# The opening of a hybrid attention layer: adaLN weights in four chunks, x transposed as it lands, small rotary tables

## The reference, cut to what matters

```python
mod = silu(c) @ w_ada + b_ada
shift, scale, gate = split(mod, 3)
h = rms_norm(x, norm_pre) * (1 + scale) + shift
proj = h @ w_in            # q, k, v, z of two attention branches, and gates
qa, ka = rope(qa, positions), rope(ka, positions)
... windowed attention (three dilations), differential attention, gated sum
y = rms_norm(y, norm_post)
return x + gate * y
```

## Time and profile before

| | us |
|---|---|
| median of 3 runs | 888.97 (888.87 to 889.76) |
| profiled execution | 890.7 |
| its span, first to last instruction | 888.9 |

### The profile page before, as it was taken

The page is one execution under the profiler, slowest core; times in us unless marked ns, Lnnn a source line. Parts: engine busy times, 40 slices in busy tenths (PEclk is TensorE's granted clock), DMA queues, the critical chain, the costliest instruction groups (busy, mean ns, idle before and its releaser), DMA issues.

```text
span 888.9 us, 12630 instructions
## 1 busy us (share of the span) xinstructions
PE 817.8 (92%) x4622; PEld 685.9 (77%) x4622; DVE 471.3 (53%) x751; ACT 360.0 (41%) x774; POOL 480.2 (54%) x625
## 2 busy tenths in 40 slices
PE   1679799999999999999997599999999999999997
PEld 0558579788888888889777477887878787888897
DVE  2884577354444545324467567857856644202622
ACT  3343444344444444433444244545555642323410
POOL 2574555344566555427767764646746527746300
PEclk9989899999999999999999699999999999999999
DMA  9774273223233433233443222223221113332521
GB/s 248 199 211 118 69 264 119 84 81 99 89 103 95 119 95 105 66 102 109 126 139 111 80 82 78 60 72 105 63 72 57 63 48 95 113 101 88 196 93 51
DMA packets 92852, 94.87 MB, mean 107 GB/s; under 512 B 8269, under 2 KB 84086, under 8 KB 92662
## 3 DMA queue, kind: packets, MB, share of 16 engines
q1 hardware_dynamic: 92496, 93.64, 34.8%
q0 software_dynamic: 240, 0.39, 0.5%
q10 hardware_dynamic: 54, 0.02, 0.0%
HBM read 78.21 MB, written 5.34 MB: 94 GB/s over the span
## 4 chain that ended last, share of the span: by engine, by line
PE 66%; POOL 9%; DVE 8%; issue 6%; DMA 5%; ACT 4%; SPq 3%; DVEq 0%; POOLq 0%; ACTq 0%
PE proj L1502 46%; POOL w_lo L694 5%; PE score L1381 4%; PE proj L1580 4%; PE sums L1427 3%; PE turned L1398 3%; DMA ada<-in_w_ada 2%; PE score L1356 2%; PE sums L1429 2%; DVE ada_sum L1025 1%; POOL rope_x L719 1%; DVE dstat L1145 1%; ACT junk L923 1%; ACT probs L891 1%; POOL rows_in L752 1%
## 5 line engine op out<-in xcount | busy, mean ns | idle before, releaser
L694 POOL TENSOR_TENSOR w_lo<-raw,w_hi 128x256 fp32r<-128x256 f32 x392 | 319.4, 846 | 218.6 <-ACT w_hi L807 218.3
L1502 PE MATMUL proj<-h_hi,w_hi 128*128 128x512 f32 x608 | 253.2, 416 | 8.3 <-POOL h_lo L704 7.1
L1502 PE MATMUL proj<-h_hi,w_lo 128*128 128x512 f32 x608 | 241.8, 398 | 0.0
L1502 PE MATMUL proj<-h_lo,w_hi 128*128 128x512 f32 x608 | 240.4, 395 | 0.0
L1502 PEld LDWEIGHTS proj<-h_hi,w_hi 128*128 128x128 f32 x608 | 116.3, 191 | 44.4 <-issue 9.9
L1502 PEld LDWEIGHTS proj<-h_hi,w_lo 128*128 128x128 f32 x608 | 116.1, 191 | 26.3
L1502 PEld LDWEIGHTS proj<-h_lo,w_hi 128*128 128x128 f32 x608 | 116.9, 192 | 21.1
L807 ACT ACTIVATE w_hi<-raw 128x1024 fp32r<-128x1024 f32 x100 | 104.2, 1053 | 11.9 <-PE proj L1502 7.7
L719 POOL TENSOR_TENSOR rope_x<-rope_x,cos_t 128x512 f32<-128x512 f32 x36 | 55.0, 1529 | 87.7 <-DMA rope_s<-rope_x 87.7
L1168 DVE TENSOR_TENSOR at_lo<-turned,at_hi 128x512 fp32r<-128x512 f32 x64 | 44.0, 688 | 63.7 <-ACT at_hi L909 63.2
L891 ACT ACTIVATE probs<-score,dstat 128x512 f32<-128x512 f32 x64 | 43.4, 684 | 60.6 <-DVE dstat L1145 60.6
(11 more groups left out here) (245 smaller groups left out, 1531.3 us busy)
## 6 DMA issues: line engine op xcount, KB each, us to landing
raw<-in_w_in SPq DMA_DIRECT2D x88, 512.0 KB, 3.6
rope_s<-rope_x SPq DMA_DIRECT2D x144, 64.0 KB, 2.4
ada<-in_w_ada SPq DMA_DIRECT2D x16, 512.0 KB, 6.3
zd<-in_w_ada SPq DMA_DIRECT2D x8, 512.0 KB, 5.6
raw<-in_w_proj_b SPq DMA_DIRECT2D x8, 512.0 KB, 3.4
raw<-in_w_out SPq DMA_DIRECT2D x8, 512.0 KB, 4.2
rows_in<-window_rows SPq DMA_DIRECT2D x4, 792.0 KB, 4.7
window_rows<-rows_out SPq DMA_DIRECT2D x4, 528.0 KB, 4.9
```

Of the source, the lines that this page charges most:

```text
L694: ins = nc.gpsimd.tensor_tensor(lo[:, k, :], raw[:, n % RAW, k, :], hi.bitcast(F32)[:, k, :], ALU.subtract)
L1502: ins = mm(dst, left, right, start=k == 0 and n == 0, stop=k == nk - 1 and n == 2)
```

## The change: four chunks, early transposes, small tables

- `w_ada` (scale and shift) comes in four chunks of 256 channels, each as eight DMAs of 256 KB in runs of 1 KB, each with its own semaphore. There is memory for all four; the last one lies where x was, so SyncE waits for `x_turned` of all eight rows before it. VectorE adds a 128 x 512 piece per instruction in place, 29 of them; three pieces of chunk 0 go to TensorE as four small matmuls each. The folding is four matmuls per chunk.
- All of x is first on SyncE's queue. Each tile is normalized after its own statistics and its transposes follow at once into seven PSUM banks; rows 2 to 7 are copied to SBUF (`xt`), and ScalarE makes `h_hi` and `h_f` from there.
- After a chunk TensorE does its two rows k for the q and k tiles and, for k 0 to 3, for the four v tiles too, which now live in the two score banks. Of the v tiles, ticks 8 to 11 keep k 4 to 7. The last two rows go pair by pair, and the swap DMAs too.
- Six halves have their own raw slots; block 3 is prepared in the opening, in memory of its own.
- Positions come as 32 frequencies x 4 quarters of 128 positions, so the angle instructions and the Sins are 128 x 128; the tables go out to DRAM and come back in eight DMAs. The lambda vectors go behind the last chunk on SyncE's queue, and their VectorE work moves to the head of ticks 12 and 24.
- G_TICK is 36 in place of 14.

```diff
-    G_TICK = 14
+    G_TICK = 36
+    N_CH, PE_ADA = 4, (2, 5, 7)
...
-    for q in ((0, 0), (1, 0), (0, 1), (1, 1), (2, 0), (2, 1)):
+    for q in ((0, 0), (1, 0), (2, 0), (0, 1), (1, 1), (2, 1), (3, 0), (3, 1)):
...
+            for tt in range(NT):
+                sp.dma_start(x_in[:, tt, :], x[0, tt * P:(tt + 1) * P, :]).then_inc(x_loaded[tt], 16)
+            for kk in range(KT):
+                load_ada(0, kk)
+            for n in range(RAW):
+                load_half(n)
+            for kk in range(4):
+                load_ada(1, kk)
+            sp.wait_ge(act_sin, 3)
+            sp.dma_start(trig_rows.rearrange("q f a n -> (q f) a n"), trig).then_inc(trig_stored, 16)
+            for kk in range(4, KT):
+                load_ada(1, kk)
+            sp.wait_ge(trig_stored, 16)
+            for i in range(4):
+                for table, a in ((cos_t, 2), (sin_t, i % 2)):
...
+            for kk in range(KT):
+                load_ada(2, kk)
+            sp.wait_ge(mod_done, 1)
             load_half(3)
+            load_half(4)
+            sp.wait_ge(x_turned, KT)
+            for kk in range(KT):
+                load_ada(3, kk)
+            load_half(5)
+            for i, v in enumerate((lambda_q1, lambda_k1, lambda_q2, lambda_k2)):
+                sp.dma_start(lam_in[:, i, :], v[0].partition_broadcast(P)).then_inc(small_loaded, 16)
...
+            for kk in range(KT):
+                sum_ada(2, kk)
+            modulate(2)
+            sum_ada(3, 0)
+            sum_ada(3, 1)
+            h_rest(4)
+            sum_ada(3, 2)
+            sum_ada(3, 3)
+            h_rest(5)
+            for kk in range(4, KT):
+                sum_ada(3, kk)
+            modulate(3)
+            h_rest(6)
+            h_rest(7)
...
+                if t == 12:
+                    lambda_dots()
...
+            for k in (0, 1):
+                first_products(qk0, k)
+            pe.wait_ge(xt_act, 3)
+            x_turn(7, range(NT))
+            first_products(v0, 0)
+            modulation(1)
+            first_products(v0, 1)
+            for k in (2, 3):
+                first_products(qk0, k)
+            first_products(v0, 2)
+            modulation(2)
+            first_products(v0, 3)
+            first_products(qk0, 4)
+            modulation(3)
+            first_products(qk0, 5)
+            for pair in (qk0[0:2], qk0[2:4]):
+                for k in (6, 7):
+                    first_products(pair, k)
```

More of the change, by code:

```diff
@@ L702, in _ @@
[L702 to L709, removed]
+                    cut_slice(n, k)
+            for part in FIRST_LO[:2]:
+                for n, k in part:
+                    pool.wait_ge(w_hi_done, n + 1)
+                    cut_slice(n, k)
@@ L931, in cut_y @@
                 nc.scalar.activation(yd_at(0, n), zd[:, n, :], ACT.Copy).then_inc(yd_hi_done, 1)
-            for tile in tiles[:4]:
-                rope_copy(tile)
-            act.wait_ge(angle_done, 1)
-            nc.scalar.activation(sin_t[:], rope_s, ACT.Sin).then_inc(act_sin, 1)
-            act.wait_ge(angle_done, 2)
-            nc.scalar.activation(cos_t[:], rope_o[:], ACT.Sin).then_inc(act_sin, 1)
+            for pair in range(2):
+                cut_hi(halves[6 + pair])
+                for tile in tiles[2 * pair:2 * pair + 2]:
+                    rope_copy(tile)
             n_y = 0
@@ new lines, in modulate @@
+            def modulate(ch):
+                ks = slice(2 * ch, 2 * ch + 2)
+                at = lambda first: cols[:, first + 2 * ch:first + 2 * ch + 2]
+                dve.wait_ge(mod_done, ch + 1)
+                link(tt_(ab[:, 0, ks], sums[:, 4 * ch:4 * ch + 2], at(16), ALU.add))
+                link(stt(out=ab[:, 0, ks], in0=ab[:, 0, ks], scalar=1.0, in1=at(32), op0=ALU.add, op1=ALU.mult))
+                tt_(ab[:, 1, ks], sums[:, 4 * ch + 2:4 * ch + 4], at(8), ALU.add).then_inc(ab_done, 1)
@@ new lines, in _ @@
+            sum_ada(0, DVE_ADA[0][-1])
+            modulate(0)
+            sum_ada(1, 0)
+            h_rest(0)
+            sum_ada(1, 1)
+            h_rest(1)
+            for kk in range(2, KT):
+                sum_ada(1, kk)
+            modulate(1)
+            for kk in range(KT):
[7 more added lines that the diff above has]
+            h_rest(5)
@@ new lines, in ada_piece, with modulation @@
+            def ada_piece(kk):
+                pe.wait_ge(ada_loaded[0][kk], 16)
+                for side in (1, 0):
+                    for k in range(2):
+                        mm(column(0, side, k), ada[0][:, kk, side, k * P:(k + 1) * P], silu_c[:, 1, kk:kk + 1],
+                           start=kk == PE_ADA[0] and side == 1 and k == 0, stop=False, skip_group_check=True)
+            def modulation(ch):
+                pe.wait_ge(ada_used, ADA_SUMS[ch])
+                if ch:
+                    pe.wait_ge(ab_done, ch)
+                for side in (1, 0):
+                    for k in range(2):
+                        ins = mm(column(ch, side, k), ada[ch][:, 0, side, k * P:(k + 1) * P], ones[:, 0:1],
+                                 start=ch > 0, stop=True, skip_group_check=True)
+                ins.then_inc(mod_done, 1)
```

447 lines of the change are left out of this document (274 added, 173 removed).

## The result

| | us |
|---|---|
| changed kernel, median of 4 runs | 880.26 (877.28 to 882.34) |
| kernel before, beside it, median of 4 | 889.37 (888.87 to 891.56) |
| ratio | 0.9894, 95% interval 0.9871 to 0.9916 |
| profiled execution, its span | 880.51, 878.6 |

Faster, as forecast, by half of the amount: 10.2 us against the profiled execution of before where 19.7 were forecast. The median of 880.3 also lies above the forecast range of 860 to 879.

The account below looks back on a forecast made before the run. Bound: TensorE's own work from tick 14, so only s0's start can move. Sum: -16.7 (products) - 4.1 (swap) + 1.7 (lambda) - 0.7 (gate pieces) = -19.7, from 890.7 to 871.0, median 869.3; range 860 to 879.

Parts of the forecast that it names:

- What bounds the kernel: Whole kernel: TensorE's own work from tick 14 on, so only the time at which that work begins can move the end.
- s0: Start of the first score on TensorE; forecast at 83.5 us against 102.55 before, 19.0 us earlier.
- Loads: Opening DMAs: 330 GB/s for 1 KB runs; x lands at 9 us, chunk 0 at 16, chunk 3 at 45.5.
- Statistics and transposes: Opening: they need x only, end near 15 us and hide behind chunk 0's load, as do the 28 small matmuls.
- VectorE sums: Opening, chunks 1 to 3: 128 x 512 sums at 1.2 us beside busy GpSimd, else 0.7; `ab` of chunk 3 at 52.5.
- my list of 10, 8 and 4: GpSimd's 24 slices in the opening: ten before chunk 1, eight from 41 us, four after half 5.
- The third rival: Opening: sums cost 1.5 us per 128 x 512, `ab` of chunk 3 near 61, time 878; chance 0.17.
- Products: TensorE, last q and k rows after `ab` of chunk 3: three times 3.07 us, less 0.1 each, plus 1 for clock.
- T: End of the q and k products on TensorE; forecast at 62 us against 78.7 before, 16.7 us earlier.
- Rotary chain: From T to s0: swap gains 4.1 us, VectorE still needs 16.1, `lambda_dots` adds 1.7; TensorE stands nearly 10 us.
- After s0: Gate pieces moved from tick 14 to 36: 0.7 us saved on TensorE, their new place costed at nothing.

Follow-up runs that it names:

- e2: Changed kernel with VectorE normalizing x tiles 0 and 1 and copying the columns before the angle instructions; 878.35 us, ratio 0.9881.
- e4: Changed kernel with all eight pieces of chunk 0 summed by VectorE and none taken by TensorE; 880.78 us, ratio 0.988.
- e6: Changed kernel with VectorE's first sum of the next chunk placed ahead of `modulate`; 878.1 us, ratio 0.9856.
- e1: Changed kernel with GpSimd writing zeros in place of the subtractions that cut the first eight weight halves; 876.49 us, ratio 0.9837.
- e0: The changed kernel as it is, measured in a second series; 880.29 us, ratio 0.988.
- e3: Changed kernel with G_TICK back to 14, all else as changed; 879.01 us, ratio 0.9871.
- e8: Kernel before with G_TICK 36 and nothing else of the change; 893.06 us against 890.12, ratio 1.0029.
- e5: Changed kernel with TensorE also taking 1, 1 and 3 pieces of chunks 1, 2 and 3; 881.99 us, ratio 0.9887.

## Why the prediction was wrong

**What bounds the kernel** was read rightly: s0 came 9.3 us earlier, the span got shorter by 10.3.

**Loads**: right. x landed in time; the earlier trace rows had 283 GB/s with 512 B runs, the changed kernel moves 340 in 14.7 to 26 us, mostly in 1 KB runs, where I took 330. By the rule of the Trainium skill ("DMA: Bandwidth & Descriptors", Specifications) that 512 B is enough for line rate, the longer runs would have brought nothing; the two stretches speak against it, though other traffic in them differs as well. For the time it made no difference, since VectorE never waited for them.

**Statistics and transposes "hide the same way"**: this step failed. They end at 23.9, not 15, for three reasons: VectorE's order (e2, 3.7 us at s0), TensorE's pieces between transposes (e4, 3.3), and TensorE's lower level, at which the transposes and pieces took 10.9 us where e6, with the higher one from 17.3 us on, took 7.1. The four 128 x 1 matmuls of a piece take 1.57 us start to start, more than the six transposes between two of them (1.31), and at the higher level 0.82 and 0.69; I had costed them at nothing, behind chunk 0's load. `ab` of chunk 0 came at 27.9, and VectorE's chunk 1 started 5.9 us after the forecast 22.

**VectorE sums**: the contended 1.2 was right (1.155), its share was not. I mixed 1.2 and 0.7, because I had ten of GpSimd's slices done before chunk 1 (and my list of 10, 8 and 4 leaves two of the 24 out). One was, since ScalarE's first cut stood behind the copies of the late transposes; nine came beside chunk 1, and each engine slows the other. With that came two waits that I had left out, 1.2 to 2.0 us per chunk for the fold and 2.1 for the first `h_f`. From `ab` to `ab`, chunk 1 took 14.1 us for 10, chunk 2 12.0 for 9, chunk 3 12.5 for 11.5: 8.1 us in sum. With the 5.9 of the start that is the whole 14.0 by which `ab` of chunk 3 was late, 66.5 for 52.5. The third rival had 61, six tenths of this delay, with another mix: 1.5 us for every sum, where the traces have a late start, more sums at 1.15 and the two waits. The Trainium skill ("SBUF — State Buffer", Who interferes with whom) says that a VectorE instruction with two SBUF inputs contends with a GpSimd one that reads SBUF, not with one that only writes. Its section "Summary: rules for kernel authors" adds that the second one to issue is blocked until the first has finished. The first agrees with e1 (752 ns beside memsets, 1043 beside subtractions). Of the second the trace shows less: a sum is 0.75 alone, a subtraction 0.74 (the median of all 376), and in lockstep both start every 1.14 to 1.16 us, not every 1.49.

**Products**: from `ab` to T 8.9 us against 9.5 (the terms that I had named, three times 2.97 and 1, make 9.9); right, with 1.1 us of lower clock in it (the first twelve matmuls take 4.14 us, later ones 3.1) where I took 1. T was 75.4 for 62.

**Rotary chain**: the swap was 1.1 us better than forecast (first sin product 2.6 after T), VectorE took 15.3 us where 17.8 had been set, lambda work included, which cost 0.4 and not 1.7 (two dot products of 0.21 and 0.23 where the earlier trace rows had 0.716). Those 3.6 us and the 0.6 of the products made up for part of the 14: s0 at 93.2 for 83.5. The wait before it was 6.5 us, not 10; the stall did not grow in the rotary chain to twice its size, and 5.71 us of it stood before the fold of chunk 3.

**After s0**: the sum was right by luck (785.4 for 785.7; 787.2 in e0) and both parts wrong. Taking the pieces out of tick 14 is worth more than 0.7: from s0 to 223 us the lead grows by 2.8 us, and by 0.3 with G_TICK 14 (e3), so the move gives 2.5 there (e8: 1.7). Putting them at tick 36 costs 4.5 us (e8: 5.4, e5: 7.1), where I had said nothing; TensorE waits 1.8 us in those ticks, where I had named no wait at all as a sign of being right. I had looked only at whether the load would be late, and at idle time of VectorE, not at GpSimd beside it. A third part, 1.5 to 2.4 us that every kernel with the new opening but e5 gains between 501 and 724 us, was in no step; in the kernel before, 535 to 550 us have a granted clock of 0.89, in e3 1.00. That was not tested.

## What to carry to other kernels

In an opening written by hand, follow every engine's program order from its first instruction: work that "needs x only" is as late as whatever is queued ahead of it, and small matmuls of one column are not free between transposes. Price TensorE's first work at its lower level: in twelve of the fourteen traces here the rise came only between 28 and 38 us. Price operations of VectorE and GpSimd that read SBUF side by side at the contended duration, and when work is moved into a stretch where VectorE has idle time, ask what GpSimd's work beside it will then take. Fix the earliest delay first and share a bound over two engines second. Expect longer waits of TensorE to cost clock as well: in the changed kernel it stood at 0.50 from 41.3 to 44.7, 61.8 to 68.6 and 89.1 to 99.3 us, around or behind its waits of 1.25, 5.7 and 6.5 us, and not behind the one of 0.52.

## What the runs showed of the hardware

- TensorE's opening ran at 1.2 GHz up to 34.5 us in the changed kernel and up to 17.3 in e6 (four transposes in 1.06 us and in 0.60), and the stretch view prints 1.00 before the first clock record.
- Eight one-column matmuls of the trace with 128 x 128 weights take 1.57 us from the first start to what follows at the lower level (changed kernel, 17.33), 0.20 each, and 0.82 at the higher (e6, 18.66), 0.10 each. Both times that is more than six transposes of 128 columns, 1.31 and 0.69. The eight of a fold take 1.84 and 1.05.
- VectorE's sums and GpSimd's subtractions, which both read SBUF, slow each other: 0.75 to 1.04 us for the sum (1.15 from start to start), 0.74 to 1.18 for the subtraction. Beside a GpSimd memset the sum takes 0.75 (e1).
- An in-place sum that waits for its predecessor costs 0.10 us more than one that does not (six in 5.03 us in e1, at 0.75 each).
